# Picks of the hidden values at eight a group of gathers, one-hots two batches ahead, an eighth row buffer

## Time and profile before

| | |
|---|---|
| median of three runs | 2126.8 us |
| the profiled execution | 2125.0 us, span 2123.0 us |
| busy in the span: TensorE, VectorE, ScalarE, GpSimd | 95%, 71%, 38%, 39% |
| granted TensorE clock, mean | 0.911 |
| chain that ended last | TensorE 77%, DMA 9%, VectorE 6% |

### The profile page before, as it was taken

How to read it: one execution, slowest core, us unless ns; L and a number is a source line. 1 busy time by engine, 2 the same in 40 slices (tenths; PEclk the granted TensorE clock), 3 DMA queues, 4 the chain that set the end, 5 groups by cost and what they waited for, 6 DMA issues and landing times.

```text
span 2123.0 us, 27862 instructions
## 1 busy us (share of the span) xinstructions
PE 2019.5 (95%) x10247; PEld 1707.7 (80%) x10247; DVE 1508.4 (71%) x1987; ACT 815.0 (38%) x956; POOL 835.2 (39%) x626
## 2 busy tenths in 40 slices
PE   7999999999999999999999979997889999999997
PEld 6988998777888889988888757765556888888886
DVE  5465774556655557688888746666635999999998
ACT  4354433444434443222221223335436444444444
POOL 1001320000000001266654565566621888888782
PEclk9999999999999999999999965555559999999999
DMA  6555443445555565699999977677732999999996
GB/s 203 188 182 182 147 151 129 159 159 165 187 183 179 199 218 195 238 409 409 408 394 364 367 272 247 220 252 253 275 119 89 379 395 395 390 406 395 394 381 239
DMA packets 176353, 558.12 MB, mean 263 GB/s; under 512 B 19152, under 2 KB 22240, under 8 KB 175200
## 3 DMA queue, kind: packets, MB, share of 16 engines
q1 hardware_dynamic: 117744, 288.47, 38.6%
q0 software_dynamic: 58480, 267.94, 33.6%
HBM read 551.62 MB, written 4.72 MB: 262 GB/s over the span
## 4 chain that ended last, share of the span: by engine, by line
PE 77%; DMA 9%; DVE 6%; issue 3%; ACT 2%; POOL 2%; SPq 0%; DVEq 0%; POOLq 0%; ACTq 0%
PE acc L1918 7%; PE acc L1920 7%; PE acc L1919 7%; PE scr L2222 6%; PE acc L2180 5%; PE scr L2180 5%; PE acc L1901 4%; PE acc L1903 4%; PE acc L1904 4%; PE scr L2252 3%; DMA v_raw<-in_v_dense 3%; DMA ub<-in_u_dense 3%; PE acc L2306 3%; PE scr L2307 3%; PE acc L2307 3%
## 5 line engine op out<-in xcount | busy, mean ns | idle before, releaser
L1104 DVE TENSOR_TENSOR w_lo<-raw,w_hi 128x2048 fp32r<-128x2048 f32 x136 | 314.6, 2314 | 279.2 <-ACT w_hi L751 278.1
L751 ACT ACTIVATE w_hi<-raw 128x2048 fp32r<-128x2048 f32 x136 | 260.1, 1913 | 405.0 <-PE acc L1920 273.5
L707 POOL DMA_INDIRECT starts<-in_v_gather,expert x256 | 366.3, 1431 | 100.1 <-DVE X L1823 76.1
L684 POOL DMA_INDIRECT slots<-in_u_gather,expert x256 | 245.4, 959 | 269.2 <-DVE slots L1623 77.3
L1623 DVE SCALAR_TENSOR_TENSOR slots<-slots,acc 128x1280 f32<-128x1280 f32 x192 | 281.8, 1483 | 79.8 <-DMA slots<-in_u_gather,expert 78.2
L1042 ACT ACTIVATE v_hi<-v_raw 128x1344 fp32r<-128x1344 f32 x128 | 170.5, 1332 | 259.5 <-PE scr L2308 197.5
L1823 DVE SCALAR_TENSOR_TENSOR X<-starts,weight,X 128x704 f32<-128x704 f32 x256 | 242.1, 946 | 0.8 <-DMA starts<-in_v_gather,expert 0.4
L1918 PE MATMUL acc<-w_hi,hT_hi 128*128 128x512 f32 x576 | 227.6, 395 | 2.5 <-DVE w_lo L1104 2.5
L1919 PE MATMUL acc<-w_lo,hT_hi 128*128 128x512 f32 x576 | 225.3, 391 | 0.0
L1920 PE MATMUL acc<-w_hi,hT_lo 128*128 128x512 f32 x576 | 225.2, 391 | 0.0
L1840 DVE TENSOR_TENSOR v_lo<-v_raw,v_hi 128x1344 fp32r<-128x1344 f32 x128 | 199.3, 1557 | 8.8 <-issue 6.7
(11 more groups left out here) (322 smaller groups left out, 4003.6 us busy)
## 6 DMA issues: line engine op xcount, KB each, us to landing
raw<-in_w_in SPq DMA_DIRECT2D x88, 1024.0 KB, 5.1
v_raw<-in_v_dense SPq DMA_DIRECT2D x128, 672.0 KB, 7.5
ub<-in_u_dense SPq DMA_DIRECT2D x128, 384.0 KB, 7.2
raw<-in_w_o SPq DMA_DIRECT2D x16, 1024.0 KB, 5.1
raw<-in_peer_wq SPq DMA_DIRECT2D x16, 1024.0 KB, 5.3
raw<-in_w_a_up SPq DMA_DIRECT2D x8, 1024.0 KB, 5.0
raw<-in_w_b_up SPq DMA_DIRECT2D x8, 1024.0 KB, 5.1
slots<-in_u_gather,expert POOLq DMA_INDIRECT x256, 7.0
```

What stands on the lines that cost most here:

```text
L684: pool.indirect_dma_start(slots[j][:, :], None, u_gather[:, :], bass.IndirectOffsetOnAxis(ap=expert[:, t, k:k + 1], axis=0)).then_inc(row_ ...
L707: pool.indirect_dma_start(starts[j][:, :], None, v_gather[:, :], bass.IndirectOffsetOnAxis(ap=expert[:, s // NSEL, s % NSEL:s % NSEL + 1], ...
L751: a.activation(w_hi[:, m % 2, :, :], raw[:, m % 2, :, :], ACT.Copy).then_inc(hi_ready, 1)
L1104: v.tensor_tensor(w_lo[:, m % 2, :, :], raw[:, m % 2, :, :], w_hi[:, m % 2, :, :].bitcast(fp32), ALU.subtract).then_inc(lo_ready, 1)
```

## The change

- `selected(i)` gives eight picks (PICKS) to each group from group 32 on, so groups 32 to 39. The hidden curve of t=0 moves from groups 43 and 44 to 38 and 39, the gate's turn from 47 to 41, the spread of the first 32 scatters from group 50 to 46. VectorE puts two finds behind each place of a group.
- ScalarE: the evictions come first in a group, ahead of the exponential of the gate and the tanh. At i = 31 it also evicts the last two pairs and writes one-hots 0 and 1, and copies h2 to PSUM after that. In later groups its one-hots are those of two batches ahead (AHEAD), two of them ahead of the row sum; the row sum is that of the group before.
- Row buffers: an eighth one (115 KiB, `NORM_ROW`, open from q = 140, once GpSimd's products of t=0 are done). The two at the end open from q = 148. `rows_b` has two buffers, not three; all are set to one at the end of group 30.
- The residual of t=0 is added after scatter 33, and each half of X has its own semaphore. GpSimd loads the second half of X once the picks are done and `hidT` is turned, not after scatter 55. Five value gathers are issued ahead of the last stage, not four, two of them early. SP loads v blocks 0 and 1 together and no longer waits for scatter 59.
- The unused `warm` products, zero long, and an unused semaphore are taken out.

```diff
@@ -51,9 +51,9 @@
 G1_AT, G0_AT = 32, 128
-ROW_AT = (32, 37, 42, 128, 133, 138, 48, 53, 58, 144, 149, 154, 107, 3, 8, 16, 21, 26, 192, 109)
-SEM_OF = (0, 1, 2, 3, 4, 5, 6, 7, 8, 9, 10, 11, 12, 8, 11, 13, 7, 10, 6, 9)
-FIRST_ROWS, HELD_ROW, SCORE_ROWS, ALL_ROWS, END_ROWS = (0, 1, 2, 11), 12, (15,), (13, 14, 16, 17), (18, 19)
+ROW_AT = (32, 37, 42, 128, 133, 138, 48, 53, 58, 144, 149, 154, 107, 3, 8, 16, 21, 26, 192, 109, 115)
+SEM_OF = (0, 1, 2, 3, 4, 5, 6, 7, 8, 9, 10, 11, 12, 8, 11, 13, 7, 10, 6, 9, 2)
+FIRST_ROWS, HELD_ROW, SCORE_ROWS, ALL_ROWS, END_ROWS, NORM_ROW = (0, 1, 2, 11), 12, (15,), (13, 14, 16, 17), (18, 19), 20
 UB_AT = (112, 120, 101, 104)
@@ -63,23 +63,24 @@
 CRING = 7
-STARTS_AHEAD = 4
-STARTS_BEFORE = 1
+STARTS_AHEAD = 5
+STARTS_BEFORE = 2
 WIDE_FROM = 10 * CRING
 RAWS = 3
 PIECES = 4
 GATE_AT = (GROUPS // 2 - 4, GROUPS - 6)
 CEN_GROUP = (13, 28)
 DVE_ALONE = range(100, 116)
-SELECT_FROM, SELECT_END = 34, 50
-MERGE_AT = 43
-GATE_TURN = 47
-SPREAD_FROM = SELECT_END
+SELECT_FROM, PICKS = 32, 8
+MERGE_AT = 38
+GATE_TURN = MERGE_AT + 3
+SPREAD_FROM = 46
 RPIECES = 3
-RA_AT, RB_AT = (31, 31.5, 199), (13, 120, 197)
+RA_AT, RB_AT = (31, 31.5, 199), (13, 99)
+AHEAD = 2
+RESIDUAL_AT = 33
 CHUNKS = 2 * NT * P // (4 * SC)
 R_ROWS = 1 + 4 * SC
 TOKENS_R = 4 * SC
@@ -142,7 +143,7 @@
         return FOUR <= q < P
-    return q >= (60 if j in SCORE_ROWS else 112 if j in ALL_ROWS else 144)
+    return q >= (60 if j in SCORE_ROWS else 112 if j in ALL_ROWS else 140 if j == NORM_ROW else 148)
@@ -175,10 +176,8 @@
-    if not SELECT_FROM <= i < SELECT_END:
-        return range(0)
-    per = NT * BATCHES // (SELECT_END - SELECT_FROM)
-    return range(per * (i - SELECT_FROM), per * (i - SELECT_FROM + 1))
+    first = max(0, PICKS * (i - SELECT_FROM))
+    return range(min(NT * BATCHES, first), min(NT * BATCHES, max(0, first + PICKS * (i >= SELECT_FROM))))
...
@@ -544,8 +543,8 @@
-                if h >= RPIECES:
-                    old = 4 * (h - RPIECES) + 4
+                if h >= RPIECES or h == len(RB_AT):
+                    old = 4 * (h - (len(RB_AT) if h < CHUNKS // 2 else RPIECES)) + 4
                     if old <= NT * BATCHES:
@@ -557,7 +556,7 @@
                     if h < CHUNKS // 2:
-                        sp.dma_start(rows_b[h % RPIECES][32 * r + 1:32 * r + 5, :].rearrange("c (s k) -> c s k", s=SC),
+                        sp.dma_start(rows_b[h % len(RB_AT)][32 * r + 1:32 * r + 5, :].rearrange("c (s k) -> c s k", s=SC),
                                      r_keep[t, s, :, :].rearrange("s c k -> c s k")).then_inc(r_landed[h % RPIECES], 16)
@@ -567,10 +566,9 @@
             sp.wait_ge(cen_stored, 16 * NT)
+            sp.wait_ge(ones_ready, 1)
+            sp.sem_inc(granted_w, 1)
             for h in range(CHUNKS):
-                if h < 2:
-                    sp.wait_ge(ones_ready, h + 1)
-                    sp.sem_inc(granted_w, 1)
                 load_rows(h)
@@ -578,15 +576,14 @@
             wait_rows(sp, 19)
+            wait_rows(sp, NORM_ROW)
             sp.wait_ge(product_ready, sum(map(on_pool, range(GATHERS))))
             sp.sem_inc(granted_w, 1)
             load_v(0)
+            load_v(1)
             sp.wait_ge(x_summed, 1)
             sp.sem_inc(granted_w, 1)
             load_v(2)
-            sp.wait_ge(hot_used, NT * BATCHES - 4)
-            sp.sem_inc(granted_w, 1)
-            load_v(1)
             for n in range(RAWS, BLOCKS):
@@ -680,6 +677,8 @@
                     wait_rows(pool, HELD_ROW)
+                if first_use(q) and j == NORM_ROW:
+                    pool.wait_ge(product_ready, sum(map(on_pool, range(NSEL))))
                 pool.sem_inc(granted, 1)
...
@@ -720,10 +719,10 @@
             wait_rows(pool, 14)
-            pool.wait_ge(gate_landed, NT)
-            pool.wait_ge(hot_used, NT * BATCHES - 8)
+            pool.wait_ge(hid_turned, NT)
+            pool.wait_ge(picked_ready, NT * BATCHES)
             pool.sem_inc(granted, 1)
-            pool.dma_start(X[:, 1, :], x_keep[:, 1, :]).then_inc(x_back, 16)
+            pool.dma_start(X[:, 1, :], x_keep[:, 1, :]).then_inc(x_back[1], 16)
@@ -1008,23 +1007,33 @@
             rows_to_psum(0)
             for i in range(GROUPS):
+                if 0 < i < GROUPS // 2:
+                    evict(2 * i - 2)
+                    evict(2 * i - 1)
                 if i == GROUPS // 2 - 1:
+                    for u in (2 * i, 2 * i + 1):
+                        evict(u)
+                    for b in range(AHEAD):
+                        hot_j(b)
                     rows_to_psum(1)
                 if i == MERGE_AT + 1:
                     hid_curve(0)
                 if i in GATE_AT:
                     gate_curve(GATE_AT.index(i))
-                if 0 < i <= GROUPS // 2:
-                    evict(2 * i - 2)
-                    evict(2 * i - 1)
-                for b in selected(i):
+                ahead = [b + AHEAD for b in selected(i) if b + AHEAD < NT * BATCHES]
+                for b in ahead[0:2]:
+                    hot_j(b)
+                late = i >= GROUPS // 2
+                if late and on_pool(FOUR * i - 1):
+                    sum_product(FOUR * i - 1)
+                for b in ahead[2:]:
                     hot_j(b)
                 if i == SPREAD_FROM:
                     hot_first(0)
                 for n in spread(i):
                     hot_first(n + 1)
                     scatter_out(n)
-                if on_pool(FOUR * i + FOUR - 1):
+                if i < GROUPS // 2 - 1 and on_pool(FOUR * i + FOUR - 1):
                     sum_product(FOUR * i + FOUR - 1)
             hid_curve(1)
@@ -1687,12 +1696,10 @@
-            def ones(first):
+            def ones():
                 dve.wait_ge(cen_stored, 16 * NT)
-                if not first:
-                    dve.wait_ge(u_used, BLOCKS)
-                for room in (rows_a[0], rows_a[1], rows_b[0]) if first else (rows_a[2], rows_b[1], rows_b[2]):
+                for room in (*rows_a, *rows_b):
                     last = v.memset(room[:, :], 1.0)
@@ -1770,7 +1777,8 @@
                             later_part(n)
-                    for b in selected(i)[q % FOUR:q % FOUR + 1]:
+                    n, at0 = len(selected(i)), q % FOUR
+                    for b in selected(i)[n * at0 // FOUR:n * (at0 + 1) // FOUR]:
                         find(b)
@@ -1779,10 +1787,8 @@
                         table(c, i - CEN_GROUP[1] - 1)
-                if i == CEN_GROUP[1] + 3:
-                    ones(True)
-                if i == SELECT_FROM - 1:
-                    ones(False)
+                if i == CEN_GROUP[1] + 2:
+                    ones()
                 if i in GATE_AT:
...
@@ -2198,12 +2205,7 @@
                 return (rows_a[h % RPIECES][g:g + R_ROWS, :].bitcast(f32r), table_i[g:g + R_ROWS, :], table_j[g:g + R_ROWS, :],
-                        rows_b[h % RPIECES][g:g + 5, :].bitcast(f32r), table_j[g:g + 5, 0:P])
+                        rows_b[h % len(RB_AT)][g:g + 5, :].bitcast(f32r), table_j[g:g + 5, 0:P])
...
@@ -2263,7 +2257,7 @@
                     turn_hid(0)
-                if b == 4 * (GATE_TURN - 1 - SELECT_FROM) + 3:
+                if b == min(NT * BATCHES, PICKS * (GATE_TURN - SELECT_FROM)) - 1:
                     turn_gate(0)
@@ -2286,10 +2280,10 @@
                 scatter(w)
-                if w == BATCHES + 6:
-                    pe.wait_ge(x_back, 16)
+                if w == RESIDUAL_AT:
+                    pe.wait_ge(x_back[0], 16)
                     take_residual(0, *VBANKS).then_inc(x_summed, 1)
-            pe.wait_ge(x_back, 16 * NT)
+            pe.wait_ge(x_back[1], 16)
             wait_scattered(pe)
```

More of the change, by code:

```diff
@@ L346, in build @@
         starts = [at(f"starts{n}", kib, [CW]) for n, kib in enumerate(
-            (192, 122.5, 125.25, 109.25, 105, 194.75, 197.5, 32, 34.75, 37.5, 40.25, 43, 128, 130.75))]
+            (192, 194.75, 122.5, 125.25, 109.25, 105, 197.5, 32, 34.75, 37.5, 40.25, 43, 128, 130.75))]
         ff_room = at("ff_room", 200, [2 * KB])
@@ L444, in build @@
         merged_hi, merged_split = sem("merged_hi"), sem("merged_split")
-        keys_in, gain2_in, gain_f_in, keys_copied, q_copied = sem("keys_in"), sem("gain2_in"), sem("gain_f_in"), sem("keys_copied"), sem("q_copied")
+        keys_in, gain2_in, gain_f_in, q_copied = sem("keys_in"), sem("gain2_in"), sem("gain_f_in"), sem("q_copied")
         shifted, gate_exp, expert_ready = sem("shifted"), sem("gate_exp"), sem("expert_ready")
@@ L457, in build @@
         gate_landed, gateT_ready = sem("gate_landed"), sem("gateT_ready")
-        spilled, x_back = sem("spilled"), sem("x_back")
+        spilled, x_back = sem("spilled"), [sem("x_back0"), sem("x_back1")]
         dense_ready, u_used, evicted = sem("dense_ready"), sem("u_used"), sem("evicted")
@@ L713, in _ @@
             pool.sem_inc(granted, 1)
-            pool.dma_start(X[:, 0, :], x_keep[:, 0, :]).then_inc(x_back, 16)
```

(14 more changed lines are left out.)

6 lines of the change are left out of this document (removed).

## The result

| | before | after |
|---|---|---|
| median of the runs measured together | 2125.1 us (4 runs) | 2153.4 us (4 runs) |
| profiled execution's span | 2123.0 us | 2150.3 us |
| granted TensorE clock, mean | 0.911 | 0.907 |

The changed kernel is slower, ratio 1.013 with a 95% interval of 1.010 to 1.016. The forecast was 2089 with a range of 2068 to 2140. Rival A (2158) is what came.

What follows compares the result with a forecast made beforehand. TensorE bounds the picks, nearly always busy but at clock 0.50, while DMA has room. Terms -23 (to the last dot), -5, -3 and -7 sum to -38 us on 2125.0: 2087, given as 2089 us; range 2068 to 2140.

Steps and rivals of the forecast that it cites:

- Rival A: Clock falls in the first 4 us after the column stream; all picks cost 2.75 us: +31, 2158 us; chance 0.19.
- the clock and the pick's length: Picks after the column stream: clock stays at 1.00 through 64 picks, each 1.52 us instead of 2.75, like scatter steps.
- The start's two pauses: TensorE at the column stream's end: idle 1.4 to 1.5 us in two pieces, short enough to keep clock 1.00.
- The row piece: Row-piece loads with two rows_b buffers: a stall of 0.6 us in every four picks, bounds 0 and 1.5.
- rival B: Clock falls mid-picks, at a row-piece stall or group 38 to 39; half the picks cold: -4, 2123 us; chance 0.09.
- stream's end: Evictions ahead of the gate's exponential at group 28 remove a TensorE wait and slow products: -5 us, bounds 1 and 7.
- start: From the column stream's end until picks run back to back: 2 us.
- eight groups of picks, warm / cold: Groups 32 to 39, eight picks each: 8 x 13.4 = 107 us at clock 1.00, 8 x 22 = 176 at 0.50.
- 24 further groups: Groups 40 to 63 at GpSimd's pace, 8.0 us each, bounds 7.9 and 9.1: 192 us.
- after the last dot: One scatter fewer ahead of the second hidden vector, -3 us; residual after scatter 33 instead of 38, -7 us.
- last stage: Value gathers and v loads issued earlier; the stage already starts without a gap and is full: nothing, plus or minus 2.
- the residual's part: Residual's product after scatter 33, not 38, raises the clock earlier: five steps at 1.75 us, not 3.16, -7 us.

Runs made afterwards that it cites:

- stride-only kernel: Against the 2085.0 us kernel (contiguous reads, filled start, row pieces 2 to 15 not loaded), the picks' 512-byte strided read put back: 2151.7 us, ratio 1.012.

## Why the prediction was wrong, step by step

*The step that failed* is the clock and the pick's length: "No row shows a pick at that clock. The nearest is the scatter step ... I take the picks as doing the same." Three causes were each enough to break it, shown one at a time (the second in three of four executions):
- The picks' operand is strided. A warm pick is 2.36 us, not 1.52, and with no pause ahead the clock is lost within the fourth of them (2151.7 against 2085.0 us, one edit apart). The scatter step had the same shape but not the same access pattern, and the trace prints only the shape.
- The start's two pauses. I counted them rightly (1.4 to 1.5 us; 1.49 measured) and put them "on the good side, by a few tenths". They are at the edge: the clock outlived them in one of four executions of one kernel, and in the trace of the kernel that streams one-hots. The pause of 1.84 us in the middle of the dense column stream was no yardstick for them; why it counted for less than two shorter ones is not shown. I also read one row too loosely: the fall after the gap of 2.34 us came at 501.3, not 501.6, and either way some 1.5 us after work had begun again. A clock that outlives a pause can still fall in the work behind it: here it did 1.1 us after the second pause.
- The row piece. I took a stall of 0.6 us, at most 1.5, with a landing of 2.3. Measured with warm picks: 2.94 and 3.11, and with contiguous reads and the filled start that wait alone loses the clock (2148.7 against 2085.0 us, one edit apart). In the first of these the eight small loads landed 4.5 us behind the last issue (issued up to 1236.98, used at 1241.54), while four gathers went out and the DMA engines were full (DMA share 1.00 from 1237 to 1241.5). With cold picks it hides, as forecast: the changed kernel has no such wait. A fall at a row piece was rival B's picture; with the clock gone after seven picks of 64, its time is rival A's.

Without all three the kernel takes 2085.0, so the rest of the sum was sound to within the 10 us or so that cancel there (above). No form that computes the right thing and has all three away was tried: by my reading of the code, the table takes its space from the row buffers block by block, and the layout that the contiguous read needs has no room as the kernel stands.

*Rival A's working* (8 x 22 = 176, +31, 2158) is borne out: 176 us, +27.3 in the span, 2153. Most of its 5 us too many are in the terms below.

| term | predicted | measured |
|---|---|---|
| stream's end | -5 | -4.2 |
| start | 2 | 1.95 |
| eight groups of picks, warm / cold | 107 / 176 | 176 |
| 24 further groups | 192 | 190 (1404 to 1594) |
| after the last dot | -3 - 7 | -11.6 (the residual's part was 6.9 with three picks a group) |
| last stage | 0 | -0.9 |

*What I did not see* is the better version beside it. Rival A says why cold picks should not be packed, but I priced no smaller number per group. At 2.75 us, three picks fit under one group's 8.4 us of gathers, and the rest of the change keeps its gain: 2088.8 and 2088.6 us, 1.5 to 1.8% under the kernel before. That these times equal the forecast of 2089 says nothing for the prediction, since the clock there is 0.50 in all the picks. From the stream's end to the last dot it is 300 us, against 324 before; how much of that is the eighth buffer's, and how much the earlier start of the picks, no run shows, because none takes one of them away.

*Chances.* A got 0.19 against 0.64. The only evidence for a held clock was the scatters, of which I compared one property.

## What to carry to other kernels

Before a step is taken to run at another step's pace, compare how its operands are read, not only their shape: at the slow clock the half-products of either took some 2.08 us, and at the fast one 2.00 and 1.16. A gain that hangs on TensorE's clock should be priced for the case that it falls, and the work placed so that this case loses nothing; three picks a group do that, eight do not. When an engine's work goes ahead of a stream of gathers, look at what stands behind it in every queue: here GpSimd waited 113 of 176 us for a row sum behind the one-hots, and VectorE's dots stood behind finds that waited for picks.

## What the runs showed of the hardware

- A strided moving operand (128 fp32 numbers 512 bytes apart) makes eight fp32 half-products take 2.00 us at clock 1.00 where contiguous ones take 1.16; at 0.50 both take 2.08 to 2.11.
- TensorE without a pause is not enough to keep the clock: it fell within the second strided pick in one kernel and within the fourth in another, and stayed at 0.50 through 176 us of picks at 99.8% busy. Contiguous picks kept it for 90 us without a pause. Strided ones with two dense products each kept it for over 100 us, and then lost it without a pause.
- Pauses and the clock, at 1.00 before them: 0.3 to 0.5 us in every scatter, and one of 1.30, left it up; 2.57, 2.94, 3.11 and 4.36 us were each met by a fall, during the pause or 0.3 us after it; 0.80 and 0.69 us within 2 us were followed by a fall in most traces and not in all, with one and the same kernel giving either.
- Dense work raises it: 16 dense products (5.98 us) did so in the middle of a cold stretch, as the residual's six do, and so did four scatters with two dense products each. The Trainium skill ("TensorE: Matmul & The Clock Gate", section "Why this matters for your kernels") asks for no long idle gaps; the stride-only kernel had none at all ahead of its fall and still lost the clock.
